# A hybrid decoder step with its program reordered in stages, and sample scores in column tiles

## What is computed

```python
c_q, c_kv, k_r, z_mla, q_n, cmp_kv, sel_kv, win_kv, g_br, z_nsa = split(x @ w_in)
# latent attention (MLA): 8 heads over 128 latent and 32 rotary channels
s = q_lat . ckv + q_rope . krope ;  o_lat = softmax(s * scale) . ckv
# sparse attention (NSA): 8 heads in 2 key groups, head size 64, three branches
kv_c  = compress(cmp_kv)        # blocks of 32 tokens, stride 16, two-layer net
o_cmp = softmax(q . kv_c.k) . kv_c.v          # over compressed blocks
o_sel = softmax(q_rot . k_sel) . v_sel        # over the 16 best blocks of 64 tokens
o_win = softmax(q_rot . k_win) . v_win        # over the last 512 tokens
o_nsa = g0 * o_cmp + g1 * o_sel + g2 * o_win
mixed = concat(o_mla * silu(z_mla), o_nsa * silu(z_nsa))
y = layer_norm(ALPHA * x + mixed @ w_o)
```

## Time and profile before

| | |
|---|---|
| Median of 3 runs | 668.57 us (667.38 to 675.55) |
| Profiled execution, its own time | 669.39 us |
| Its span, first to last instruction | 667.6 us |
| TensorE busy / mean granted clock | 603.6 us (90%) / 0.972 |
| VectorE, ScalarE, GpSimd busy | 288.2, 214.8, 94.3 us |
| DMA moved | 60.34 MB |

### The profile page before, as it was taken

One profiled execution on the slowest core, in us unless ns is written; L12 is line 12 of the kernel. 1 busy time (PEld: TensorE's weight loads), 2 busy tenths in 40 slices (PEclk: granted clock), 3 DMA queues, 4 the chain that ended last, 5 costly groups with the idle time before them and its releaser, 6 DMA issues. The chain is left out here.

```text
span 667.6 us, 10193 instructions
## 1 busy us (share of the span) xinstructions
PE 603.6 (90%) x3482; PEld 371.5 (56%) x3482; DVE 288.2 (43%) x758; ACT 214.8 (32%) x614; POOL 94.3 (14%) x175
## 2 busy tenths in 40 slices
PE   5989998989888999799899899999999998999995
PEld 3554553666556764454546465665575765465642
DVE  0131203262959366733445335345534455355335
ACT  1330103241442221242434243544345345153210
POOL 0114522110011224110010001021003121000000
PEclk9989999989999899969999989999999998999999
DMA  8816463476307512223403106042302701010101
GB/s 305 271 56 138 103 157 54 63 94 114 85 1 243 215 37 74 75 74 105 119 1 95 33 1 190 9 119 64 127 1 63 293 1 40 1 63 1 64 0 63
DMA packets 42381, 60.34 MB, mean 90 GB/s; under 512 B 8986, under 2 KB 34074, under 8 KB 41722
## 3 DMA queue, kind: packets, MB, share of 16 engines
q1 hardware_dynamic: 42330, 59.69, 32.6%
HBM read 55.43 MB, written 8.41 MB: 96 GB/s over the span
## 5 line engine op out<-in xcount | busy, mean ns | idle before, releaser
L830 PE MATMUL psum<-wring,bufA 128*128 128x512 f32 (+2 forms) x384 | 160.1, 567 | 2.7 <-DMA wring<-in_w_in 2.7
L830 PEld LDWEIGHTS psum<-wring,bufA 128*128 128x128 f32 x384 | 73.4, 197 | 68.1 <-issue 61.6
L1397 ACT ACTIVATE wring<-wring,small 128x128 f32<-128x128 f32 (+3 forms) x96 | 53.9, 561 | 160.3 <-DVE small L1680 160.0
L1680 DVE CUSTOM_DVE_ANT_0 wring<-psum,const 128x128 f32<-128x128 f32 (+3 forms) x96 | 46.6, 486 | 86.6 <-PE psum L1053 75.1
L804 PE MATMUL psum<-const,ring 128*128 128x128 f32 (+2 forms) x360 | 50.6, 276 | 21.7 <-ACT mid L591 8.1
L1283 PE MATMUL psum<-ring,comp 128*128 128x512 f32 x128 | 56.5, 595 | 1.5 <-issue 1.5
L804 PEld LDWEIGHTS psum<-const,ring 128*128 128x128 f32 (+2 forms) x360 | 37.5, 136 | 35.8 <-ACT mid L591 9.3
L804 PE MATMUL psum<-const,wring 128*128 128x128 f32 x272 | 49.6, 280 | 6.8 <-ACT wring L1476 3.9
L1053 PE MATMUL psum<-mid,qrT 128*128 128x128 f32 (+3 forms) x128 | 50.2, 475 | 3.8 <-DVE small L1674 3.8
L804 PEld LDWEIGHTS psum<-const,wring 128*128 128x128 f32 x272 | 34.2, 143 | 33.6 <-issue 18.5
L1084 PE MATMUL psum<-kv,wring 128*128 128x64 f32 x320 | 43.8, 268 | 1.0 <-DVE rtmp L1708 0.8
(11 more groups left out here) (227 smaller groups left out, 791.3 us busy)
## 6 DMA issues: line engine op xcount, KB each, us to landing
wring<-in_w_in SPq DMA_DIRECT2D x4, 2048.0 KB, 9.8
ring<-in_cache_cmp_kv SPq DMA_DIRECT2D x64, 128.0 KB
ring<-in_cache_mla SPq DMA_DIRECT2D x64, 80.0 KB, 1.8
ring<-in_cache_sel_kv SPq DMA_DIRECT2D x40, 128.0 KB, 2.1
ring<-in_state_win_kv SPq DMA_DIRECT2D x8, 512.0 KB, 5.4
ring<-in_w_o SPq DMA_DIRECT2D x1, 4096.0 KB, 13.7
out_s_win<-in_state_win_kv SPq DMA_DIRECT2D x1, 4064.0 KB
wring<-in_cache_sel_kv SPq DMA_DIRECT2D x24, 128.0 KB, 2.0
```

What stands on the lines that cost most here:

```text
L830: ins = pe.matmul(bank[:, 0:w], xT[:, c, t * P:(t + 1) * P], wr[:, b % 2, c, 0:w], start=(c == 0), stop=(c == KC - 1))
L1397: ins = act.activation(Pp[:, n % 4, 0:w], Pp[:, n % 4, 0:w], ACT.Exp, bias=nmp[:, k, h:h + 1], scale=-1.0, accum_out=lp[:, k, h:h + 1])
L1680: ins = dve.tensor_tensor_reduce(Pp[:, n % 4, 0:w], bank[:, 0:w], mask, -(MLA_SCALE if kind == "pmla" else NSA_SCALE), CLAMP, ALU.add, ALU ...
```

## The change

The list of steps is put in another order, and several buffers move so that this order is possible.

- Blocks are projected in the order latent, compression, queries, window, ZNSA, ZMLA. The compression is woven with the rest of the first four blocks. The two gate blocks are woven with the prompt's sparse attention, sample attention with the prompt's latent attention; the output of the first tiles with the last eight units and a few more.
- A sample `score` step does all four samples of an item for one half of 1024 keys: four matmuls of 32 query rows follow each other into the four groups of 32 PSUM partitions of one bank. The rotary part is one matmul over 128 rows (4 samples x 32 channels, `qrope` being block-diagonal). `keys` and `rkeys` steps transpose the keys of two samples at a time.
- `padK` goes. A prompt score contracts the 64 rows of its own key group, heads of both groups alternate (`HEADS`), and units go in pairs: both scores, then the transposes and values of earlier pairs (lags 4 and 6).
- SP's order of loads follows; `w_o` is loaded in four parts, since its ring is used longer.

```diff
-BLK = [(CUTS[0], CUTS[3] - CUTS[0]), (CUTS[4], MW), (CUTS[5], 2 * KVW), (CUTS[3], MW),
-       (CUTS[7], KVW + 3 * H), (CUTS[9], MW)]
-B_MLA, B_Q, B_CMPSEL, B_ZMLA, B_WINGATE, B_ZNSA = range(6)
+BLK = [(CUTS[0], CUTS[3] - CUTS[0]), (CUTS[5], 2 * KVW), (CUTS[4], MW), (CUTS[7], KVW + 3 * H),
+       (CUTS[9], MW), (CUTS[3], MW)]
+B_MLA, B_CMPSEL, B_Q, B_WINGATE, B_ZNSA, B_ZMLA = range(6)
...
-KINDS = ("pcmp", "psel", "pwin", "pmla")
+KINDS = ("psel", "pwin", "pcmp", "pmla")
+HEADS = [g * HG + hh for hh in range(HG) for g in range(G)]
...
-T_LAG, V_LAG = 3, 5
+T_LAG, V_LAG = 4, 6
...
+    steps += weave(halved(products[first:dense]), cmp)
...
+    def pair(m):
+
+        a, b = slot(m, 0, N_NSA), slot(m + 1, 0, N_NSA)
+        k = int(m < N_NSA)
+        return a[:k] + b[:k] + a[k:] + b[k:]
+
+    z = halved(products[dense:]) + [([("zrecip", *seq[-1])], .1), ([("qup_s",)], 1)]
+    p = [(pair(m), cost(m) + cost(m + 1) if m < N_NSA else 1) for m in range(0, N_NSA + V_LAG, 2)]
+    steps += weave(z, p)
...
+        body.append(([("min", *x, 0)], 0))
+        if BANKS_OF[x[0]] == 2:
+            body += keys_of(x, 1)
         if last:
             body.append(([("pv", *last)], 2))
...
+        body += [([("new", *x)], .5), ([("least", *x)], .5)]
+        ahead = keys_of(nxt, 0) if nxt else []
+        body += ahead[:1] + [([], .5), ([("exp", *x)], 1)] + ahead[1:] + [([("norm", *x)], 1.5)]
...
+    beside = len(p) - H - V_LAG
+    steps += weave(s, p[:beside])
...
+    steps += weave([([step], 7 if step[0] == "out" else 1) for step in out], p[beside:])
...
             load_x(4)
-            load_w(2)
             sp.wait_ge(page_in, 16)
             load_chunks(0)
+            load_w(2)
+            load_chunks(1)
...
             load_w(3)
-            load_chunks(1)
             load_chunks(2)
+            load_chunks(3)
...
+            load_chunks(4)
             load_w(4)
-            load_chunks(3)
             load_w(5)
...
             for what, k, last in LOADS:
                 if last is None:
-                    wait_full(sp, A, A.at("proj", B_ZNSA, NT - 1))
+                    wait_full(sp, S, S.at("pscore", N_NSA - 1))
+                    sp.wait_ge(bd_ready, 1)
...
-            wait_full(sp, O, O.at("pv", "sel", NG - 1))
-            sp.dma_start(wo, io["w_o"][0].rearrange("(c p) n -> p c n", p=P)).then_inc(wo_in, 16)
+            sp.wait_ge(sel_read, NG)
+            for c in (2, 4, 6):
+                load_wo(c, 2, wo_in[1])
...
+            def turn_keys(rope, kind, g, half, two):
+
+                for b in (2 * two, 2 * two + 1):
+                    if half == 0 and not rope:
+                        if kind == "mla":
+                            pe.wait_ge(m_land[g * GB + b], 16 * PAGES)
+                        else:
+                            what = (kind, g, b if kind == "sel" else b // 2)
+                            pe.wait_ge(r_land[SLOT_OF[what]], ring_landed(what))
...
+            def score(kind, g, half):
...
+                u = A.at("score", kind, g, half)
+                bank = claim(A, u)
+                q = qlatT if kind == "mla" else qrbd
+                for b in range(GB):
+                    ins = pe.matmul(bank[b * RB:(b + 1) * RB, :], q[:, g * P + b * RB:g * P + (b + 1) * RB],
+                                    kt[:, b, :], start=True, stop=True)
+                if kind == "mla":
+                    ins = pe.matmul(bank, qrope[:, g * P:(g + 1) * P], krp, start=False, stop=True,
+                                    skip_group_check=True)
+                ins.then_inc(A.full[u % A.n], 1)
...
                     g, hh = h // HG, h % HG
-
-                    ins = pe.matmul(bank[:, 0:keys], qrT3[:, hh, q], padK[:, int(kind == "pwin"), g, 0:keys],
-                                    start=True, stop=True)
+                    s, kT = slice(g * HD, (g + 1) * HD), selKT if kind == "psel" else winKT
+                    ins = pe.matmul(bank[:, 0:keys], qrT3[s, hh, q], kT[s, 0:keys], start=True, stop=True)
...
```

More of the change, by code:

```diff
@@ L207, in chunks, with slot, cost, keys_of @@
             return ([("chunks", t + 1, k, half)], 1) if t + 1 < NT else ([], 1)
-        cmp += [([("hid", t, 0)], 2), ([("cmpout", t - 1)] if t else [], 1), chunks(0, 0), ([("hid", t, 1)], 2),
+        cmp += [([("hid", t, 0)], 3.5), ([("cmpout", t - 1)] if t else [], 1), chunks(0, 0), ([("hid", t, 1)], 3.5),
                 chunks(0, 1), ([("hexp", t)], .5), chunks(1, 0), ([("hsilu", t)], .5), chunks(1, 1)]
     cmp.append(([("cmpout", NT - 1)], 1))
[L212 to L218, removed]
+    steps += weave(halved(products[first:dense]), cmp)
+    def slot(m, lo, hi):
+        now = []
+        if m < hi:
+            now.append(("pscore", m))
+        if lo <= m - T_LAG < hi:
+            now.append(("pturn", m - T_LAG))
+        n = m - V_LAG
+        if lo <= n < hi:
+            now.append(("pvalue", n))
+            if n + 1 == hi or UNITS[n + 1][:2] != UNITS[n][:2]:
+                now.append(("branch", *UNITS[n][:2]))
+        return now
+    def cost(m):
+        i, kind, _ = UNITS[m]
+        return 1.5 if kind == "pcmp" else 0.47 * (i + 1) + .5
+    def pair(m):
[5 more added lines that the diff above has]
+    steps += weave(z, p)
     def compressed(g):
         return [([(k, g)], 1) for k in ("cscore", "cexp", "cnorm", "cturn", "imp0", "imp1", "drop")]
+    def keys_of(x, half):
+        kinds = ("keys", "rkeys") if x[0] == "mla" else ("keys",)
+        return [([(k, *x, half, two)], 1.3) for k in kinds for two in range(2)]
+    s = [([("bd",)], .1), ([("qhead",)], 1), ([("wuk", 0)], 1), ([("wuk", 1)], 1)]
+    s += keys_of(ITEMS[0], 0)[:2] + [([("qlat",)], 1.5)] + keys_of(ITEMS[0], 0)[2:]
     for n, x in enumerate(ITEMS):
@@ L319, in t_uses @@
         return 2 if a[0] == B_Q else 1
-    if kind == "keys":
-        return min(2, KEYS_T[a[0]] - 2 * a[3])
+    if kind in ("keys", "rkeys"):
+        return 2
     if kind == "probs":
@@ L1905, in _ @@
             for step in STEPS:
-                if step[0] == "qup_s":
+                kind, a = step[0], step[1:]
+                if kind == "proj" and a[0] not in (B_ZMLA, B_ZNSA):
+                    turns += 1
+                    rope_block(*a, turns)
+                elif kind == "zrecip":
+                    silu(*a)
+                elif kind == "qup_s":
                     for half in range(2):
-                        wait_copied(pool, B, B.at(*step) + half)
+                        wait_copied(pool, A, A.at(*step) + half)
```

502 lines of the change are left out of this document (238 added, 264 removed).

## The result

The changed kernel takes 690.03 us (median of 4 runs, 686.33 to 701.11) beside 671.05 for the kernel before on the same chip: a ratio of 1.026, with a 95% interval of [1.016, 1.036]. The forecast was 652 us, faster; the time lies outside its range. Ratios leave out executions that were disturbed, so they can differ a little from those of the medians; the profiled one of the first experiment was such a one. The profiled execution took 686.33 us, its span 684.4.

What follows compares the result with a forecast made beforehand. TensorE's work was taken to set the time, with SP's page loads late next: 545 work + 50 old idle + 56 page waits + 2 clock = 653 us span, 654 as median, less 2 gives 652 us; 8-in-10 range 622 to 680.

Steps and rivals of the forecast that it cites:

- TensorE's work, 545: TensorE's busy time over the whole kernel: 603.6 us less 41 and 18 saved in the scores gives 545 us.
- Column tiles 41: Sample scores: four samples follow each other in four column groups, saving 38 to 45 us, taken as 41.
- row halves 18: Prompt selection and window scores: 64-row matmuls overlap in pairs, gaining 11 to 26 us, taken as 18.
- rival 1: Prompt scores: row halves do not overlap, 18 us back, 670 us; chance 0.18.
- The pages, 56: TensorE's new waits for cache pages in compression, selection and window items: 56 us, SP ending the longest.
- the walk: Count, along the new order of steps, of TensorE's work between SP's release to load and the first use.
- Rival 2: Pages do not hold TensorE as counted: 596 us without the 56, 624 with half; chance 0.24.
- Of the old idle time I keep about 50: TensorE's small waits over all stages: of the old 64 us, about 50 stay beside the page waits.
- rival 4: All of the old 64 us of idle time stays beside the new waits: 14 more, 666 us; chance 0.08.
- 6 with the latent attention: Old idle time kept in the stage with the latent attention: 6 us of the 50.
- I add 2 us: Lower granted clock after idle time, with five long waits in place of several short ones: 2 us added.
- I take 2 off: Other engines catch up while TensorE waits for pages, sparing a few small waits: 2 us off 654.

Runs made afterwards that it cites:

- the first experiment: Changed kernel with the third and fourth chunk set loaded ahead of the window weights: 671.09 us, ratio to before 0.991.
- both repairs of the issue: Changed kernel with chunk sets loaded ahead of the window weights and page numbers of selection loads read ahead by SP: 660.39 us, ratio to before 0.985.
- With most of its pages in time: Changed kernel with chunk sets ahead of the window weights and page numbers written into the program, look-up left out: 653.58 us, ratio to before 0.975.
- the useless products: Identity matmuls without use put before waits for pages: in the changed kernel 715.49 us; with early chunk sets and page numbers read ahead 653.88 us.
- the last run: Changed kernel with early chunk sets, page numbers read ahead and 16 useless matmuls before six page waits of sample attention: 653.88 us, ratio to before 0.975.

## Why the prediction was wrong

The span was forecast at 653 us and is 684.4. By the prediction's own terms:

- **TensorE's work, 545, right.** Column tiles 41 forecast and 42 measured in busy time, row halves 18 (bounds 11 to 26) and 23. At full clock, work fell by 57 us; forecast 59. Busy time as such is 561.4, over the 560 that was named as the sign of rival 1. The sign misled: the surplus is time at half clock, and rival 1 falls by the run without pairs. A pair of the last tile and a group of four sample scores took 1.1 us of busy time each, forecast 0.9.
- **The pages, 56, right in sum and not in its parts.** Compression 13 forecast, the long wait 21.0: the walk gave a chunk set 25 us from release to landing by SP's issue, and it took 32.5 to its use, because the transfer and not the issue ends it. Selection 37 forecast, 30.4 measured; windows 6.1 and 6.6. Together 60, +4. Rival 2 falls.
- **"Of the old idle time I keep about 50": failed.** 123 us of idle time less 60 for the pages leave 63, the old 64 almost whole. This is rival 4, which had a chance of 0.08: +13. By stage, idle time without the page waits is 9, 12, 7, 20 and 15 us, against the 10, 9, 9, 6 and 16 that the prediction kept. So the miss lies in one term, "6 with the latent attention", the stage where sample attention now runs: 20. There TensorE waits for the small steps of the sample's own chain, above all for the copy that builds the block-diagonal `qrope` (L1793), the scaling of the sample's probabilities (L1654) and the copies of its transposed keys (L1401):

```profile
PE psum L834 <- DVE bufA L1793: 3.4, 1, 3.4
PE psum L834 <- DVE bufA L1654: 3.2, 2, 2.1
PE psum L834 <- ACT w1h L1401: 2.6, 4, 1.0
```

  Of the 14 us that the prediction struck from the old sum it had rows for 7 (3.8 and 3.3, which went but for 0.6).
- **"I add 2 us" for the clock: failed.** Work at half clock cost 30 us against 15: +13. Of the 30, 15 lie in the stage of sample attention and 8.5 in that of the compression, the two stages with the page waits.
- **"I take 2 off" for the other engines: failed**, nothing was spared.

2 (work) + 4 (pages) + 13 + 13 is the miss of 31 in the span to within a microsecond. The median lies 3.7 us above the profiled execution where before it was 0.8 below: another 4.5, and with the 2 taken off, 38.

What the runs show of the cause: the waits for pages are an effect of the new order and most of the loss. Taking 39 us of idle time out with two edits on SP's queue alone brings 690 to 660. Column tiles alone in the old order give 644, so the loss is not in them. With most of its pages in time the changed kernel stands at 654, with 16 us less work than four column tiles in the old order need for 646. It packs the stage with the gates to 95% busy and leaves the sample's stage, after both repairs of the issue, at 132 of 171 us and a clock of 0.90. Two things stay open. One is how much the lost clock lengthens the kernel by itself: the useless products took about as much time as the clock gave back, and in the last run they hardly moved it. The other is how much of the lost clock comes from the order of stages and how much from the pairs and row halves. In the old order these lowered the clock, in the new order leaving the pairs out lowered it further, and no run has the new order without them and with its pages in time.

## What to carry to other kernels

Take the time of an order from its thinnest stage: when work is gathered into one dense stage, what is left in the other must still cover its loads and its own chain of small steps. Before moving stages, try the cheap half of a change in the old order; here some 20 lines gave 4%, and the change as a whole, with its reordering, took all of it back. Carry the old idle time over whole unless each microsecond struck off has a row, expect more of it in a stage that gets thinner, and price work beside short waits at the clock that such stretches have in the trace.

## What the runs showed of the hardware

- In fp32, four column tiles of 32 columns and two row halves overlap almost fully when they are neighbours in the queue: 58.1 us busy became 14.9 (four tiles in the old order), and 51.1 without pairs became 27.1 with them.
- A kernel with less TensorE work can run at a lower clock while it is busy: with 11 us less work, and its units in pairs, 93 us of busy time were at half clock in place of 32.
- A page whose number SP has read ahead takes it 0.5 us (16 in 8.1), against 1.1; as a number in the program 0.5 (16 in 7.45) or 0.4 (32 in 12.06).
- Faster issue need not land pages sooner: the third chunk set was used 30.9 us after SP's release with numbers in the program and 32.5 with look-ups.
